# A decoder trunk on one core: work moved between engines at the start, in the last down projection and at the end, and 18 and 15 tiles of weight sums

## Chip, cores and metric

One core of a Trainium2 chip runs the whole program. The metric is the device time of one execution in microseconds; the time given for a kernel is the median of its runs. Engines are named as in the profile: PE (TensorE), DVE (VectorE), ACT (ScalarE), POOL (GpSimd) and SP (SyncE, which issues nearly all DMAs).

## What is computed

x is 2048 tokens by 1024; one layer, fp32 throughout.

```python
mod = (silu(c) @ ada_w + ada_b); sh1, sc1, g1, sh2, sc2, g2 = split(mod, 6)
h = rmsnorm(x, norm1_g) * (1 + sc1) + sh1
x = x + g1 * hybrid_mixer(h, ...)       # w_in 1024 x 4624, SSD scan by chunks of 128, gMLP, w_out 2048 x 1024
h = rmsnorm(x, norm2_g) * (1 + sc2) + sh2
x = x + g2 * conv_gated_ffn(h, ...)     # ff_up 1024 x 5632, causal conv of width 3, silu, ff_down 2816 x 1024
return rmsnorm(x, final_g)
```

## The kernel before

The tokens go in four blocks of 512 (b = 0 to 3, four tiles t of 128). `mixer(b)` runs for each block, and after each odd one `ffn(s)` runs for two blocks at once (s = 0, 1). Each engine's program is written out by hand, in order, with semaphores between them; an engine that waits holds all that is behind it, and SP's order of DMAs is part of it.

A product in fp32 is made of fp32r parts: a weight tile of 128 x 512 is loaded (`w_raw`), ACT rounds it to `w_hi` (`split`, L750), POOL subtracts (`low`, L646), and PE takes hi x hi, hi x lo and lo x hi. One such tile with four 128-wide steps of the other operand is a unit: 12 matmuls of 512 columns. A ring of four slots holds the units. In mixer 0 the split weights are also stored to DRAM (`store_split`), and mixers 1 to 3 load them back, 512 KB a unit (`hl_d`, L378). A mixer has 104 units: 24 for x, B and C of the SSD part (j = 0 to 2, with a conv on DVE after each eight), 32 for the gMLP inputs with the four chunks of the scan between them, 16 for z, 32 for the output projection (j = 0, 1).

The ffn uses a seven-product scheme for 2 x 2 blocks (P1 to P7). For it, POOL makes 33 tiles of weight sums (`t_step`, four subtractions or additions, L657) from four loads each, and SP stores them (`t_store`): tiles 0 to 21 for the up, 22 to 32 for the down projection. `T_OF` says that 20 of them are made in mixer 1 and 13 in the first up projection, `T_AT` at which unit each is loaded. The up projection has 154 units, the down projection 77 (P1, P2, P6, P7, P4, P5, P3 with 11 each); there both the weight and the activation (`a_high` on ACT, `low` on DVE, L1469) are split.

The start: x and small rows are loaded by ACT's queue, the adaLN weights (`ada_w`, slabs of 1 MB) by SP's. DVE multiplies the slabs by silu(c) and adds them (`ada_sum`, L1112), PE sums over partitions into columns (`mod_column`, L1770), and h_hi and h_lo of the first block follow from them (`h_tiles` on ACT; `h_lo` by POOL for the first `HF0` = 4, L664, by `h_lows` on DVE for the rest). The dt projection (L1864) comes after the first eight units.

The end of mixer 0: gate rows of the adaLN weights are summed, PE adds them up (L2022), DVE adds the bias (L1436), and only then `norm_x` takes the statistics of the next block and scales it (L1057 to L1096), for the transposes on PE (L1761).

The end of the program: POOL multiplies y by the gate (`final_step`, L678), DVE adds it to x, takes bn statistics, makes the reciprocal root in 12 small steps (`rms_rstd`); for half 1 POOL multiplies by the gain and ACT scales, for half 0 DVE does both (L1714), and the tiles are stored.

## Time and profile before

| what | us |
|---|---|
| median of 3 runs (2843.17 to 2851.38) | 2846.13 |
| the profiled execution | 2852.3 |
| its span, from the first to the last instruction | 2850.4 |
| PE busy in it | 2705.3 (95%) |
| DVE, POOL, ACT busy | 1849.8, 1094.9, 983.9 |

In the profile a busy time is that of the records of an engine; matmuls overlap, so PE counts as busy also where it runs slower than it could. The granted clock is a share of full speed (1.00 is 2.4 GHz, 0.50 is 1.2 GHz). Stretches are named by their start and end in us from the span's start.

### The profile page before, as it was taken

What the parts mean: (1) busy time and instruction counts of PE and PEld (TensorE: products, weight loads), DVE (VectorE), ACT (ScalarE), POOL (GpSimd) and SP (SyncE); (2) the same over time, 40 slices, a digit from 0 to 9 for tenths busy, and PEclk for the clock granted to TensorE, in tenths of its full rate; (3) what the DMA queues carried; (4) which work ended last, traced back from release to release, by engine and by line L of the source; (5) the groups of instructions that cost most, each with busy time, mean ns of one, the idle gap of its engine ahead of it and who ended that gap; (6) DMA issues with size and microseconds to landing.
All of it is one profiled execution on the core that took longest, in us unless ns stands there. A gap on an engine that the chain in (4) does not pass through costs nothing.

```text
span 2850.4 us, 33659 instructions
## 1 busy us (share of the span) xinstructions
PE 2705.3 (95%) x12363; PEld 2207.4 (77%) x12363; DVE 1849.8 (65%) x2610; ACT 983.9 (35%) x1472; POOL 1094.9 (38%) x736
## 2 busy tenths in 40 slices
PE   3899989899999999999999999999999999999994
PEld 3778868688777888877878888888887888887783
DVE  5777955658467656568786466555737745456868
ACT  2453333322143333344534212233114433334342
POOL 3344431545137777644560000000004544444455
PEclk8899999999999999999999999999999999999997
DMA  9587777999755665573447546665464444437343
GB/s 349 188 299 280 258 266 230 352 350 326 262 183 181 219 210 189 184 280 89 159 153 254 177 156 237 196 221 186 144 225 156 128 126 126 123 110 281 89 131 123
DMA packets 252063, 584.02 MB, mean 205 GB/s; under 512 B 25621, under 2 KB 83449, under 8 KB 247803
## 3 DMA queue, kind: packets, MB, share of 16 engines
q1 hardware_dynamic: 250662, 579.54, 59.9%
q8 instruction: 98, 1.61, 0.2%
q10 hardware_dynamic: 1238, 2.34, 0.2%
q14 instruction: 65, 0.53, 0.1%
HBM read 448.48 MB, written 133.31 MB: 204 GB/s over the span
## 4 chain that ended last, share of the span: by engine, by line
PE 72%; DVE 10%; DMA 7%; POOL 4%; issue 4%; SPq 2%; ACT 1%; DVEq 0%; ACTq 0%; POOLq 0%
PE main L1798 30%; PE pair L2069 14%; PE main L2069 14%; PE main L2083 4%; PE pair L2083 4%; POOL tb L657 2%; DMA t_up_scratch<-tb 2%; DMA tb<-in_ff_up_dram 2%; DVE a_lo L1469 2%; PE pair L1936 1%; DMA w_split_scratch<-w_hl 1%; POOL w_hl L646 1%; DVE mod_sum L1112 1%; SPq L431 1%; SPq L439 1%
## 5 line engine op out<-in xcount | busy, mean ns | idle before, releaser
L646 POOL TENSOR_TENSOR w_hl<-w_raw,w_hl 128x512 fp32r<-128x512 f32 x568 | 828.7, 1463 | 1551.8 <-ACT w_hl L750 1549.5
L750 ACT ACTIVATE w_hl<-w_raw 128x512 fp32r<-128x512 f32 x568 | 355.2, 630 | 867.8 <-PE main L2069 177.8
L1798 PE MATMUL main<-w_hl,h_hi 128*128 128x512 f32 x1536 | 493.6, 403 | 6.3 <-DMA w_hl<-w_split_scratch 5.4
L1798 PEld LDWEIGHTS main<-w_hl,h_hi 128*128 128x128 f32 x1536 | 285.0, 189 | 78.9 <-issue 16.5
L1798 PE MATMUL main<-w_hl,h_lo 128*128 128x512 f32 x768 | 300.9, 392 | 0.0
L657 POOL TENSOR_TENSOR tb<-tb,tb 128x512 f32<-128x512 f32 x132 | 206.2, 1562 | 169.2 <-DMA tb<-in_ff_up_dram 164.5
L1798 PE MATMUL main<-h_hi,w_hl 128*128 128x512 f32 x768 | 250.6, 401 | 11.8 <-POOL h_lo L664 5.4
L1469 DVE TENSOR_TENSOR a_lo<-g,a_hi 128x512 fp32r<-128x512 f32 x132 | 184.1, 1403 | 101.7 <-ACT a_hi L971 101.4
L2083 PE MATMUL main<-w_hl,a_hi 128*128 128x512 f32 x704 | 224.5, 401 | 18.1 <-DVE a_lo L1469 15.4
L2069 PE MATMUL pair<-s_hi,w_hl 128*128 128x512 f32 x736 | 235.7, 393 | 2.4 <-POOL w_hl L646 2.4
L2069 PE MATMUL main<-s_hi,w_hl 128*128 128x512 f32 x672 | 215.5, 394 | 1.9 <-DVE s_lo L1462 1.2
L1532 DVE SCALAR_TENSOR_TENSOR c_acc<-c_gate,col_b,c_acc 128x512 f32<-128x512 f32 x176 | 210.7, 1237 | 3.9 <-ACT c_acc L937 1.5
L1798 PEld LDWEIGHTS main<-h_hi,w_hl 128*128 128x128 f32 x768 | 147.3, 192 | 44.2 <-POOL h_lo L664 5.5
L2083 PEld LDWEIGHTS main<-w_hl,a_hi 128*128 128x128 f32 x704 | 132.8, 192 | 56.7 <-issue 16.7
L1798 PEld LDWEIGHTS main<-w_hl,h_lo 128*128 128x128 f32 x768 | 144.6, 188 | 31.6
L2069 PEld LDWEIGHTS pair<-s_hi,w_hl 128*128 128x128 f32 x736 | 138.2, 188 | 35.5 <-POOL w_hl L646 3.2
L2083 PE MATMUL pair<-w_hl,a_hi 128*128 128x512 f32 x528 | 163.2, 390 | 1.5 <-DVE a_lo L1469 1.3
L1798 PE MATMUL main<-w_hl,gmT_hi 128*128 128x512 f32 x512 | 159.7, 393 | 4.3 <-DMA w_hl<-w_split_scratch 4.3
L2069 PEld LDWEIGHTS main<-s_hi,w_hl 128*128 128x128 f32 x672 | 126.2, 188 | 33.4 <-issue 2.9
L1798 PE MATMUL main<-h_lo,w_hl 128*128 128x512 f32 x384 | 151.9, 396 | 0.0
L1798 PE MATMUL main<-w_hl,yT_hi 128*128 128x512 f32 x480 | 148.5, 390 | 0.0
L2069 PE MATMUL pair<-s_lo,w_hl 128*128 128x512 f32 x368 | 144.6, 393 | 0.0
(268 smaller groups left out, 4908.8 us busy)
## 6 DMA issues: line engine op xcount, KB each, us to landing
w_hl<-w_split_scratch SPq DMA_DIRECT2D x312, 512.0 KB, 3.9
w_split_scratch<-w_hl SPq DMA_DIRECT2D x104, 512.0 KB, 5.8
w_raw<-t_up_scratch SPq DMA_DIRECT2D x176, 256.0 KB, 2.7
w_raw<-in_ff_up_dram SPq DMA_DIRECT2D x132, 256.0 KB, 3.5
w_raw<-t_down_scratch SPq DMA_DIRECT2D x90, 256.0 KB, 2.6
tb<-in_ff_up_dram SPq DMA_DIRECT2D x88, 256.0 KB, 4.6
t_up_scratch<-tb SPq DMA_DIRECT2D x88, 256.0 KB, 5.5
g_scratch<-c_val SPq DMA_DIRECT2D x44, 512.0 KB, 4.0
```

The lines of the kernel that those rows point to most:

```text
L431: sp.dma_start(k_pair(dst), up_quarter(which, t // 2, t % 2)).then_inc(t_ld[m], 16)
L439: sp.dma_start(dst, tb[t_set(t)][which][:]).then_inc(t_st[t_set(t)], 16)
L646: nc.gpsimd.tensor_tensor(w_lo[:, g % RING, :], w_raw[:, g % RING, :], w_hi[:, g % RING, :].bitcast(F32), ALU.subtract).then_inc(w_lo_ok, 1)
L657: nc.gpsimd.tensor_tensor(dst, one, other, how).then_inc(t_add, 1)
L750: nc.scalar.activation(w_hi[:, g % RING, :], w_raw[:, g % RING, :], ACT.Copy).then_inc(w_hi_ok, 1)
L1112: V.scalar_tensor_tensor(out=dst, in0=piece, scalar=c_act[:, k:k + 1], in1=dst, op0=ALU.mult, op1=ALU.add).then_inc(ada_summed, 1)
L1469: V.tensor_tensor(a_lo[j % RING][:], full_a, a_hi[j % RING][:].bitcast(F32), ALU.subtract).then_inc(a_lo_ok, 1)
L1532: last = V.scalar_tensor_tensor(out=piece, in0=c_gate[q % 2][:, i, lo:lo + BT], scalar=col_b[:, R_FW + tap * KF + m:R_FW + tap * KF + m + ...
L1798: ins = T.matmul(main[i], a, w, start=first and p == 0, stop=last and p == 2)
L1936: last = T.matmul(aux[2 + h // (NH // 2)][:, o:o + HD], arow[:, h, :], xdt[:, h * HD:(h + 1) * HD], start=True, stop=True)
L2069: ins = T.matmul(got[:, i, :], w[:, kl, cols], a[:, k, :], start=k == 0 and m == 0, stop=k == KH - 1 and m == 2)
L2083: ins = T.matmul((main, aux)[p % 2][i], a, w[:, s_w, :], start=k == 0 and m == 0, stop=k == KG - 1 and m == 2)
```

## The change

- Start: x is loaded by SP ahead of the adaLN weights. PE multiplies the first two slabs by silu(c) directly (`mod_direct`), so DVE sums six; the columns are made and finished in two halves; h_lo of tiles 0 and 1 is made by DVE, of 2 and 3 by POOL. The dt projection, its transposes, the scan and the second columns each come some units later, and three of the second sums come after the first convs.
- End of mixer 0: `norm_x` comes before the gate rows; PE's sums of these come at unit 11 of j = 0; x and the broadcast gate are loaded four units sooner; all h_lows come after the left half of the residual.
- Weight sums: 18 tiles in mixer 1 (one every 3.6 units instead of 3.2), 15 in the first up projection (one every 8.5 instead of 9.5), stored there six units after their load instead of seven.
- 35 of the weights of the last down projection (P6, one of P7, one of P4, P5 and P3) are loaded, split and stored in mixers 2 and 3 (`pre_load`, `pre_high`, `pre_low`, `pre_store`) and loaded split.
- Odd mixers: the right half of the residual is multiplied by the gate in PSUM and added from there.
- Down projections: four activations are split ahead of the last conv instead of two.
- End: squares with a sum on ACT take the place of the bn statistics; POOL does all multiplications by the gate and the gain, apart from the last quarter, which DVE takes from PSUM; half 0 is scaled on ACT and DVE.

```diff
...
-        ADA_RING, ADA_FIRST, HF0 = 12, 4, 4
+        ADA_RING, ADA_FIRST, HF0, ADA_PE = 12, 4, 2, 2
...
+        PRE_J = list(range(2 * KG, 3 * KG + 1)) + list(range(5 * KG - 1, ND))
...
-        T_OF = (range(0), range(0, 20), range(20, 33))
-        T_AT = ((), [16 + 16 * i // 5 for i in range(20)], [18 + 19 * i // 2 for i in range(13)])
+        PRE_OF = {2: range(17), 3: range(17, len(PRE_J))}
+        PRE_AT = [22 + 17 * i // 5 for i in range(18)]
+        PRE_BUF = 3
+        pre_hi_ok, half_sum, sq_ok = sem("pre_hi_ok"), sem("half_sum"), sem("sq_ok")
+        T_OF = (range(0), range(0, 18), range(18, 33))
+        T_AT = ((), [16 + 18 * i // 5 for i in range(18)], [18 + 17 * i // 2 for i in range(15)])
 
...
+        PRE_G = {ffn0(NSB - 1) + DOWN + j: i for i, j in enumerate(PRE_J)}
...
-                    sp.wait_ge(ada_summed, i - ADA_RING + 1)
+                    sp.wait_ge(mod_col, 1)
...
+            for t in range(NT):
+                sp.dma_start(xn01[:, t, :] if t < 2 else xn23[:, t - 2, :], x[0, t * P:(t + 1) * P, :]).then_inc(x_in, 16)
...
+            def pre_load(i):
+                if i < 2:
+                    sp.wait_ge(t_st[i], 64 * T_IN[i])
+                else:
+                    sp.wait_ge(t_add, T_ADDS + i - 1)
+                sp.dma_start(pre_raw[i % 2][:], down_source(PRE_J[i] // KG, PRE_J[i] % KG)).then_inc(t_ld[i % 2], 16)
+
+            def pre_store(i):
+                sp.wait_ge(t_add, T_ADDS + i + 1)
+                sp.dma_start(pre_d[i], pre_hl[i % PRE_BUF][:].bitcast(F32)).then_inc(hl_st[i % PRE_BUF], 16)
...
+                if b >= 2:
+                    for i, at in zip(PRE_OF[b], PRE_AT):
+                        if n == at + 6:
+                            pre_store(i)
+                    for i, at in zip(PRE_OF[b], PRE_AT):
+                        if n == at:
+                            if i == PRE_OF[3][0]:
+                                sp.wait_ge(x2_st, 16 * NT * 3)
+                            pre_load(i)
                 if b % 2 and 11 <= n < 11 + NT:
...
-                x2_at_unit = OUT + (17 if b else 21)
+                x2_at_unit = OUT + 17
...
-                                if u == at + 7:
+                                if u == at + 6:
...
+                    g = f0 + DOWN + j
+                    if loaded(g):
+                        sp.wait_ge(w_used, g + 1)
+                        sp.dma_start(w_hl[:, g % RING, :, :].bitcast(F32), pre_d[PRE_G[g]]).then_inc(hl_in[g % RING], 16)
+                    else:
+                        load(g, down_source(p, k))
...
+                if loaded(g) or g == UNITS - 1:
+                    return
...
+            def pre_low(i):
+                pool.wait_ge(pre_hi_ok, i + 1)
+                nc.gpsimd.tensor_tensor(pre_hl[i % PRE_BUF][:, 1, :], pre_raw[i % 2][:],
+                                        pre_hl[i % PRE_BUF][:, 0, :].bitcast(F32), ALU.subtract).then_inc(t_add, 1)
...
-                        if j in FIN_AT:
+                        if s + 1 < NSB and j in FIN_AT:
...
+                    for step in range(8):
+                        final_step(s, step)
...
-            for t in range(NT):
-                act.dma_start(xn01[:, t, :] if t < 2 else xn23[:, t - 2, :], x[0, t * P:(t + 1) * P, :]).then_inc(x_in, 16)
...
+            def pre_high(b, n):
+                while b >= 2 and pre_next[0] in PRE_OF[b] and PRE_AT[pre_next[0] - PRE_OF[b][0]] + 3 <= n:
+                    i = pre_next[0]
+                    pre_next[0] += 1
+                    act.wait_ge(t_ld[i % 2], 64 * T_IN[i % 2] + 16 * (i // 2 + 1))
+                    if i >= PRE_BUF:
+                        act.wait_ge(hl_st[i % PRE_BUF], pre_stored(i - PRE_BUF))
+                    nc.scalar.activation(pre_hl[i % PRE_BUF][:, 0, :], pre_raw[i % 2][:], ACT.Copy).then_inc(pre_hi_ok, 1)
+
...
+            def squares(half, c, summed, ts=range(NT)):
+                act.wait_ge(half_sum, summed)
+                for t in ts:
+                    nc.scalar.activation(y_half[half][:, t, c * W:(c + 1) * W], x_half[half][:, t, c * W:(c + 1) * W], ACT.Square,
+                                         accum_out=sq[:, 4 * half + t, c:c + 1]).then_inc(sq_ok, 1)
...
-                    if n == NUP - 1:
+                    if n == NUP - 2:
                         a_high(0)
                         a_high(1)
+                    if n == NUP - 1:
+                        a_high(2)
+                        a_high(3)
...
+                    if s == NSB - 1 and p == P5 and k in (9, 10):
+                        squares(0, 0, 1, (2 * k - 18, 2 * k - 17))
+                    if s == NSB - 1 and p == P3 and k in (6, 7):
+                        squares(1, 0, 2, (2 * k - 12, 2 * k - 11))
+                    if (s, p, k) == (NSB - 1, P3, 8):
+                        squares(1, 1, 3)
...
-            for i in range(3):
-                ada_sum(i)
             for t in range(NT):
                 norm_stats(0, t, (xn01[:, 0, :], xn01[:, 1, :], xn23[:, 0, :], xn23[:, 1, :])[t])
             rms_rstd(NT, xr_ok)
-            for i in range(3, KD):
+            for i in range(ADA_PE, KD):
...
-            mod_columns(0, main[3], R_N1)
-            for i in range(KD, 2 * KD):
+            for half in range(2):
+                mod_columns(0, slice(4 * half, 4 * half + 4), (main[3 - 2 * half], main[2]), R_N1, 1 + half)
...
+                            link(V.tensor_tensor(main[t], main[t], g_bc[:, W:D], ALU.mult))
+                            V.tensor_tensor(x2[:, t, W:D], x2[:, t, W:D], main[t], ALU.add).then_inc(evacuated, 1)
...
+                if b % 2 == 0:
+                    norm_x(b + 1, [xnew[:, t, :] for t in range(NT)])
...
+                        low(s, 2)
+                        low(s, 3)
...
+                    xx = x_half[0][:, t, W:D]
+                    link(V.tensor_tensor(main[t], main[t], g2_bc[:, W:D], ALU.mult))
+                    V.tensor_tensor(xx, xx, main[t], ALU.add).then_inc(half_sum, 1)
...
+                rms_rstd(NT, xr_ok, 0, True)
...
+            def mod_direct(bank):
+
+                for k in range(ADA_PE):
+                    pe.wait_ge(ada_in[k], 16)
                 for m in range(2 * KD):
-                    last = T.matmul(bank[:, m:m + 1], mod_sum[:, 2 * n + m // KD, (m % KD) * P:(m % KD + 1) * P], ones,
-                                    start=True, stop=True)
-                last.then_inc(mod_col, 1)
+                    for k in range(ADA_PE):
+                        T.matmul(bank[:, m:m + 1], ada_t[:, (k + ADA_FIRST) % ADA_RING, m * P:(m + 1) * P], c_act[:, k:k + 1],
+                                 start=k == 0, stop=k == ADA_PE - 1)
 
             pe.sem_inc(w_used, RING)
...
-                        if (j, k) == ((0, 1) if b else (0, KD - 1)):
+                        if (j, k) == ((0, 1) if b else (1, 1)):
...
+                        if b == 0 and (j, k) == (1, 7):
+                            pe.wait_ge(ada_summed, 2 * KD - ADA_PE)
+                            mod_column(1, range(KD), aux[0])
...
-                        if b == 0 and j == 1 and k == 0:
+                        if b == 0 and j == 0 and k == 11:
...
+                def down_weights(u):
+                    if loaded(u):
+                        pe.wait_ge(hl_in[u % RING], 16 * ((NB - 1) * (MU // RING) + PRE_G[u] // RING + 1))
...
```

## Rows read from the trace of the kernel before

**Rows 1.** Windows: busy of PE, PEld, DVE, ACT, POOL; clock, DMA share, GB/s:

```profile
82.76:95.52 12.76, 6.58 (x17) 5.24 (x18) 5.77 (x6) 4.74 (x7) 0.08 (x1) 0.73 0.29 104
95.52:152.15 56.63, 54.15 (x246) 44.75 (x244) 35.81 (x73) 26.78 (x42) 22.42 (x16) 0.91 0.63 204
...
379.10:443.95 64.85, 55.66 (x242) 43.88 (x241) 37.52 (x63) 16.20 (x26) 18.76 (x14) 0.92 0.59 203
443.95:805.39 361.44, 347.84 (x1653) 282.95 (x1652) 218.03 (x402) 94.15 (x132) 126.24 (x82) 0.99 0.88 309
...
1241.94:1470.72 228.78, 219.09 (x957) 176.75 (x957) 176.32 (x176) 104.99 (x174) 137.50 (x89) 0.99 0.50 165
...
1811.80:2152.88 341.08, 341.08 (x1653) 281.75 (x1652) 186.44 (x403) 93.95 (x132) 3.10 (x2) 1.00 0.60 199
...
2588.69:2817.00 228.31, 218.45 (x924) 175.40 (x924) 173.42 (x154) 89.20 (x153) 124.66 (x81) 0.98 0.46 151
2817.00:2850.30 33.30, 0.00 (x0) 0.00 (x0) 28.57 (x54) 4.60 (x4) 10.60 (x4) 0.57 0.31 126
```

**Rows 2.** Chain in order of time: start, us, what, matmuls:

```profile
2690.63 29.92 PE pair L2083 x132
```

**Rows 3.** Waits of PE: total us, times, longest:

```profile
PE main L2083 <- DVE a_lo L1469: 15.4, 17, 2.9
PE main L1798 <- DMA w_hl<-w_split_scratch: 13.6, 11, 2.5
PE pair L1761 <- DVE xnew L1096: 9.2, 1, 9.2
```

**Rows 4.** Timeline of DVE and PE at the start: start, us, what [idle before]:

```profile
22.45 1.29 DVE L1057 BATCH_NORM_STATS2 stats<-xn 128x6 f32<-128x512 f32 x2 [6.75 <-DMA xn<-in_x_dram]
...
30.97 13.82 DVE L1112 SCALAR_TENSOR_TENSOR mod_sum<-ada_t,c_act,mod_sum 128x2048 f32<-128x2048 f32 x5
...
44.84 6.99 PE L1770 MATMUL main<-tri,mod_sum 128*128 128x1 f32 x32 [5.50 <-DVE mod_sum L1112]
57.27 0.80 PE L1798 MATMUL main<-h_hi,w_hl 128*128 128x512 f32 x1 [5.43 <-POOL h_lo L664]
```

**Rows 5.** Windows at the start, columns as in rows 1:

```profile
3.00:30.00 27.00, 0.00 (x0) 0.00 (x0) 13.06 (x22) 0.00 (x0) 0.00 (x0) 1.00 1.01 408
...
35.00:62.00 27.00, 15.37 (x65) 13.98 (x65) 13.46 (x8) 8.20 (x13) 17.89 (x8) 0.68 1.02 416
```

**Rows 6.** Timeline at the end of mixer 0:

```profile
384.90 1.47 DVE L1436 TENSOR_TENSOR gate_rows<-pair,gate_rows 1x512 f32<-1x512 f32 x2 [20.24 <-PE pair L2022]
...
399.50 3.65 PE L1761 MATMUL pair<-ident,xnew 128*128 128x128 f32 x16 [9.19 <-DVE xnew L1096]
```

**Rows 7.** Waits of SP in mixer 1: total us, times, longest:

```profile
SPq L431 <- DMA t_up_scratch<-tb: 41.8, 11, 5.7
```

**Rows 8.** Groups: DVE in mixer 3 and last down projection; POOL, ACT before 443:

```profile
L1366 DVE TENSOR_TENSOR y_sb<-y_sb,stage 128x512 f32<-128x512 f32 x8 | 5.0, 684 | 0.0
...
L1469 DVE TENSOR_TENSOR a_lo<-g,a_hi 128x512 fp32r<-128x512 f32 x45 | 64.8, 1446 | 34.4 <-ACT a_hi L971 34.3
...
L646 POOL TENSOR_TENSOR w_hl<-w_raw,w_hl 128x512 fp32r<-128x512 f32 x104 | 166.3, 1604 | 253.3 <-ACT w_hl L750 251.5 <-DMA w_split_scratch<-w_hl 1.4
...
L750 ACT ACTIVATE w_hl<-w_raw 128x512 fp32r<-128x512 f32 x104 | 64.7, 628 | 158.6 <-PE main L1798 79.4 <-DMA w_split_scratch<-w_hl 61.5 <-issue 17.6
```

**Rows 9.** DVE at a down projection's start; windows of the last one:

```profile
1248.61 3.45 DVE L1469 TENSOR_TENSOR a_lo<-g,a_hi 128x512 fp32r<-128x512 f32 x2
...
2650.00:2690.00 40.00, 36.91 (x152) 27.51 (x151) 35.53 (x37) 14.50 (x26) 18.00 (x13) 1.00 0.31 86
...
2745.00:2817.00 72.00, 68.11 (x289) 54.46 (x287) 58.07 (x43) 25.39 (x44) 52.06 (x28) 0.98 0.43 150
```

**Rows 10.** Timeline of DVE and POOL in the tail:

```profile
2821.11 10.60 POOL L687 TENSOR_TENSOR x_half<-x_half,fg_bc 128x1024 f32<-128x1024 f32 x4 [8.14 <-DVE rstd L1073]
...
2842.11 4.87 DVE L1714 SCALAR_TENSOR_TENSOR x_half<-x_half,rstd,fg_bc 128x1024 f32<-128x1024 f32 x4
```

More of the change, by code:

```diff
@@ L696, in _ @@
                 s = b // 2 - 1
+                if b == NB:
+                    for i in range(len(PRE_J)):
+                        pre_low(i)
                 if b % 2 == 0:
@@ L1249, in mixer @@
                         kx = 4 * j + i
+                        if b == 0 and (j, i) == (0, 2):
+                            dt_copy()
+                        if b == 0 and (j, i) == (1, 2):
+                            scan()
                         full(j, i)
@@ L1255, in mixer @@
                         dt_first()
+                        for i in range(KD + 5, 2 * KD):
+                            ada_sum(i)
+                        dve.wait_ge(a_exp, 1)
+                        link(V.tensor_scalar(small[:, 0, :], small[:, 0, :], -1.0, None, ALU.mult))
                         dt_rest()
-                        scan()
+                        dve.wait_ge(wdt_h, 2)
+                        link(V.memset(state[:], 0.0))
                     if b == 0 and j == 1:
                         acs_copy()
-                        mod_columns(1, aux[0], R_N2)
+                        mod_columns(1, slice(0, KD), (aux[0],), R_N2, 3)
                         for g in range(2):
@@ L1436, in mixer @@
                         V.tensor_tensor(row, aux[m][0:1, :], row, ALU.add).then_inc(gate_ok, 1)
-                if b % 2 == 0:
-                    norm_x(b + 1, [xnew[:, t, :] for t in range(NT)])
-                if b == 0:
-                    h_lows(1, range(4), aux, [acc[:, 0, :], acc[:, 1, :]])
                 dve.wait_ge(x2_in, 16 * (NT + 1) * (b + 1))
```

282 lines of the change are left out of this document (173 added, 109 removed).

## The prediction

> **What bounds the kernel now.** I read the stages first [rows 1]. The span, 2850.4 us, is TensorE's: in mixers 2 and 3 it is busy for all of 341.08 us. A unit is 12 matmuls; a run of 132 in the chain took 29.92 us, so 11 units at 2.72 us [rows 2]. So I look for time in which PE does not run at that pace. Five places hold it. The start: the first unit of the input projection begins at 57.27. The rest of mixer 0: 12.76 us between its first 8 units and the next one, of which the dt matmul is the work, and 64.85 us for its last 16 units. Mixer 1: 361.44 us against 341.08. The two down projections: 228.78 and 228.31 us for 77 units, which are 77 x 2.72 = 209.4. And the tail: 33.30 us after the last matmul [rows 1]. The waits name who ends three of them [rows 3]: a_lo from DVE (15.4 us in the downs), weights from the split scratch (13.6), xnew from DVE (9.2).
>
> **The start.** x (2 MB) is issued on ACT's queue beside 8 MB of adaLN weights, and DVE meets it at 22.45; then it has 5 sums left, 13.82 us from 30.97; after them 32 one-column matmuls take 6.99 us, and h_hi and h_lo another 5.43 until 57.27 [rows 4]. After the change x lands first. The queues move 408 to 416 GB/s [rows 5], so 2.1 MB take 5 us from about 4; its statistics, 8.5 us from 22.45 to 30.97 now, end at 17.5. Slabs 2 to 7 then arrive every 2.5 us until about 29.5, and a sum costs 2.8 (13.82 / 5) at most, so the sums end one after the last landing: about 32 in place of 44.8. Half of the column matmuls (8 of them, 1.7 us), three small ops (0.6), h_hi (0.8), h_lo (1.7) make 37: 20 us sooner. The direct matmuls for slabs 0 and 1 (32, at 6.99 us or less) and the row transposes run in PE's idle time before 31; even rows that land at 30 as now only bring this to about 44.
> But the queue takes over. It is full until 62 [rows 5]: 2.1 + 8.4 + 1.1 + 4.2 MB, then a weight (0.26), a split store (0.52) and a slab (1.05) for each of four units. By that the weights of units 4 to 7 land at about 45, 50, 54, 58, which the new order does not move. Unit 7 then starts at 58.3 + 0.63 + 1.6 (split on ACT and POOL [rows 8]) = 60.5 and ends at 63.2. Units 8 to 10 land at 64, 66, 68 behind the last slab and ws, and ACT evacuates the banks only after the split of unit 10: unit 8 starts at 69. It started at 95.52, after the dt matmul; that follows now at unit 9, 3.6 us at full clock, so I compare 69 + 3.6 = 72.6: 23 sooner.
> From there 56.63 us held 16 units, 43.5, and the same small transposes and columns, 7.3 [rows 1]; of the other 5.8 a 2.5 us wait goes (the scan now sits between two conv tiles, done 6 us before PE asks). Against that: PE idle from 63 to 69 starts unit 8 at the low clock, as it did behind the present gap (a granted mean of 0.73 there, and half is 1.2 GHz) [rows 1], 3.4 us, and the sums 13 to 15, now behind the conv tiles, end within 2 us of PE's call. Net 23 + 2.5 - 3.4 = **22**; bounds 12 (conv and dt work pushes DVE so far that the mixer's chunks begin late) and 27.
>
> **The end of mixer 0.** The statistics and scaling of xnew start only when the gate rows are done and end at 399.36; PE stands 9.19 us, then runs at half clock [rows 6]. Without that the part is 43.5 + two transposes of 2.4 + 1.3 = 49.6 against 64.85. The work (some 11 us: the 8.5 of statistics and four scalings) now starts at 364.7, when DVE falls idle for 20.24 us [rows 6]; hidden by it, it ends at 376. SP has to wait 4 us for the gate rows with three weights queued behind it; they have 8 us of cover. The residual of the left half now stands ahead of the first h_lows, and the broadcast lands at about 388: last h_low at 405, PE asks at 404. Gain 15 - 2 = **13**; bounds 5 and 15.
>
> **Mixer 1.** 20 tiles of weight sums become 18, 4 MB less of 112, and a tile comes every 3.6 units in place of 3.2. SP waited 41.8 us for the stores of a tile before it could load the next into the same buffers [rows 7]; the weights behind those waits are the 13.6 us of PE [rows 3]. The wider step gives a store 2.3 us more and ends most of the first wait. But 10 of the loads now fall on the unit of a store, against 3 before: 2 MB and a weight, 6.2 us at the rate of rows 5 and more until it lands, where the weight has three units, 8.2. I take **5** of the 20.4 us; bounds -5 and 12. The first up projection gets 15 tiles: POOL needs (8.5 + 4) x 1.6 = 20 of 8.5 x 2.72 = 23.1 us per tile [rows 8] and PE has 2.7 units of cover; the store one unit sooner holds SP about 4 us for POOL's last step, with a slack of 1.4 units left. **0**, bounds -2 and 0.
>
> **Mixers 2 and 3, the new work.** 35 down weights are loaded, split and stored: 35 x 0.63 us on ACT and 35 x 1.6 on POOL [rows 8], with 27 MB on queues at 0.6 [rows 1]. ACT waits in order for a load that SP issued three units before; before each evacuation it has at least one unit of cover. POOL is idle there. **0**, bounds -8 and 0. DVE's TENSOR_TENSOR takes 0.68 us in mixer 3 with POOL idle, and 1.45 in the last down projection with POOL at work [rows 8]. The Trainium skill (SBUF — State Buffer, Who interferes with whom) states that such an op with two SBUF inputs and a POOL op block each other for the whole instruction; the trace agrees. By that rule the new subtractions could push DVE in mixers that have no slack on PE: a rival below.
> The residual of odd mixers is multiplied in PSUM: three adds with two SBUF inputs, 0.68 to 1.45 each by those rows, go to 0.68, on the path to the next transposes: 0 to 2.3, **1.3** twice, since POOL is at work there.
>
> **The down projections.** a_lo 2 waited for the conv, collect and gate of the last quarter: it ran at 1248.61 for PE's unit at 1247.2 [rows 9], a stall of 2.9 and half clock behind it, 4.9 us. Now four a_lows stand ahead (to 1243); next late is the weight of unit 3, split after fsilu, at about 1250.9 against 1249.9. **3.5** each; bounds 0 and 4.9. In the second one 35 of 77 weights come split, and POOL is out of DVE's way in P6, where DVE is busy 89% and PE issues 152 matmuls in 40 us, 5.5 us short at 0.2267 each (2.72 / 12), and in P5 and P3, 289 in 72 us, 6.5 us short [rows 9]. I take **11.5** of 12; bounds 4 and 13, since POOL still does the multiplications by the gate there.
>
> **The tail.** POOL takes 10.60 us for four gains, beside which DVE's multiplications and adds of y are slow; the statistics follow, and DVE's last scale is 4.87 from 2842.11; the last store lands some 3 us behind it [rows 10]. New, from the last bank: multiply and add from PSUM 1.4 (2 x 0.68), square 0.6, the chain of the root 2.4 (estimate: the 8.5 of rows 4 less four tiles' statistics), the left half on ACT and the right on DVE 2.5 each, side by side (half of 4.87), store 2.9: 10 with semaphores. The squares of that bank stand behind half1_scale on ACT, and that behind six gains on POOL (2.65 each, from about 15 us before the end): 16. I take 14: **19** of 33.3; bounds 14 and 23.
>
> **Sum.** 22 + 13 + 5 + 0 + 0 + 2.6 + 3.5 + 3.5 + 11.5 + 19 = 80. From the profiled execution (2852.3, span 2850.4) that is 2772; its time is 6 above the median of 2846.1, so 2766 to 2772 and I say **2768**.
>
> **Rivals.**
> The serial parts move less: the start and mixer 0's end at their lower bounds, since DVE, ACT and SP run in order there: 22 + 13 becomes 17, so 2786. For: three programs are reordered at once. Against: the DMA queue, not they, sets unit 7.
> POOL in the way: each of the 35 subtractions (1.6 us) delays DVE by 1.3 us on a path to PE, 46 us: 2814. For: no PE slack in mixers 2 and 3. Against: in mixer 1 POOL is busy 126 us and PE waits for DMA alone [rows 1, 7].
> The split ahead buys nothing: DVE, not POOL, bounds P6 and P3: 11.5 falls away, 2780. For: DVE at 89%. Against: twofold times beside POOL [rows 8].
> Slower: SP meets 70 new issues in order; a pre_store waits for POOL, which waits for ACT, and every weight behind it is late. In mixer 1 a tile of sums cost 20.4 / 20 = 1.0 us of PE. Here the price would have to be over 80 / 35 = 2.3 us; at one whole unit, 2.72, it is 95: 2862. Against: mixer 1 had its queues at 0.88, here they go to about 0.7.
>
> **Chances.** Forecast 62%, less at the serial parts 16%, nothing from the split ahead 12%, POOL 5%, slower 2%, a gain beyond my upper bounds 3%. The range 2750 to 2796 reaches over the first three; POOL, slower and the gain beyond are the 10% left out, and as much again may lie in the tails of the others. Faster by over 0.3% (what a measurement of this kernel tells from no change) 0.96, within 0.02, slower 0.02.
>
> **What would show it.** First unit of the input projection near 37 to 44, the eighth near 60; the chunks of mixer 0 from about 130 in place of 152; no 9 us wait for xnew; mixer 1 near 356; mixers 2 and 3 at 341 to 343; down projections near 225 and 213; a tail of 14. A mixer 2 or 3 above 350, or a start over 50, makes it wrong.

## The result, and the profile after

| | median us (runs) | ratio to before, 95% interval |
|---|---|---|
| before | 2847.05 (4: 2843.17 to 2851.38) | |
| changed | 2815.28 (4: 2811.02 to 2823.99) | 0.9892, 0.9864 to 0.9920 |

The change makes the kernel 1.1% faster. The forecast was 2768, range 2750 to 2796: the direction was right, the size was not. Of 80 us that the sum counted, 37 came.

The windows of the changed kernel by stage, to be set against [rows 1] (length, busy of PE, PEld, DVE, ACT, POOL, clock, DMA share, GB/s). In order: start, rest of mixer 0 up to its output projection (two lines), that projection, mixer 1, first up, first down, mixers 2 and 3, second up, second down, tail:

```profile
0.00:43.02 43.02, 21.66 (x116) 21.23 (x116) 23.57 (x41) 10.22 (x15) 6.03 (x12) 0.97 0.95 369
43.02:136.37 93.35, 87.21 (x372) 71.27 (x373) 65.29 (x95) 41.84 (x65) 40.60 (x25) 0.89 0.74 268
136.37:320.83 184.46, 178.18 (x889) 144.42 (x889) 151.35 (x246) 78.66 (x120) 77.88 (x49) 1.00 0.75 267
320.83:426.60 105.77, 100.77 (x457) 80.01 (x456) 71.74 (x118) 31.22 (x51) 42.50 (x29) 0.98 0.76 275
426.60:783.51 356.91, 345.62 (x1653) 282.16 (x1652) 219.12 (x404) 94.17 (x132) 111.13 (x74) 1.00 0.85 301
783.51:1233.97 450.46, 436.30 (x1881) 347.67 (x1880) 281.85 (x242) 173.44 (x255) 305.29 (x216) 1.00 0.59 195
1233.97:1461.05 227.08, 218.52 (x958) 175.19 (x957) 174.70 (x176) 103.80 (x172) 136.52 (x89) 1.00 0.50 166
1461.05:1802.13 341.08, 341.08 (x1654) 281.67 (x1653) 220.86 (x452) 95.48 (x139) 26.62 (x17) 1.00 0.71 241
1802.13:2143.21 341.08, 341.08 (x1653) 281.62 (x1652) 192.14 (x405) 103.92 (x150) 30.31 (x20) 1.00 0.72 241
2143.21:2575.75 432.54, 429.82 (x1881) 349.76 (x1880) 256.72 (x241) 174.75 (x255) 214.31 (x155) 1.00 0.42 130
2575.75:2801.29 225.54, 216.00 (x925) 175.42 (x923) 161.11 (x161) 81.19 (x144) 97.46 (x53) 0.98 0.57 197
2801.29:2813.70 12.41, 0.00 (x1) 0.00 (x0) 6.13 (x19) 4.71 (x12) 0.00 (x0) 0.65 0.63 251
```

Read against the same stretches of before (the lengths that [rows 1] does not hold are from the same view), with the term of the sum beside it:

| stage | before | after | saved | forecast |
|---|---|---|---|---|
| up to the chunks of mixer 0 | 152.2 | 136.4 | 15.8 | 22 |
| mixer 0, chunks to output projection | 180.3 | 184.5 | -4.2 | 0 |
| output projection of mixer 0 | 111.5 | 105.8 | 5.7 | 13 |
| mixer 1 | 361.4 | 356.9 | 4.5 | 5 |
| first up projection | 436.6 | 450.5 | -13.9 | 1.3 |
| first down projection | 228.8 | 227.1 | 1.7 | 3.5 |
| mixers 2 and 3 | 682.2 | 682.2 | 0.0 | 0 |
| second up projection | 435.8 | 432.5 | 3.3 | 1.3 |
| second down projection | 228.3 | 225.5 | 2.8 | 15 |
| tail | 33.4 | 12.4 | 21.0 | 19 |
| sum | | | 36.7 | 80 |

36.7 is the difference of the spans, 2850.4 - 2813.7. Two stages hold most of what is missing: the first up projection (15.2) and the second down projection (12.2); mixer 0 as a whole gives 17.3 in place of 35.

The waits of PE, of the whole changed kernel (total us, times, longest), beside [rows 3]:

```profile
PE main L2246 <- DVE a_lo L1606: 12.4, 14, 4.2
PE pair L2226 <- POOL w_hl L703: 7.6, 13, 2.3
...
PE main L2226 <- POOL w_hl L703: 4.8, 9, 1.4
PE pair L1903 <- ACT xn L808: 4.7, 1, 4.7
```

The wait for xnew is gone. New are the waits of the up projection (L2226) for weights, 12.4 us in all, where before had 3.0. And a_lo still holds PE for 12.4 us, against 15.4, in another place: 8.5 us of it lie in four waits of the last product, one of 4.2.

In the last product of the down projection (P3) the timelines of DVE and POOL show how:

```profile
2777.18 4.49 DVE L1813 TENSOR_TENSOR x_half<-x_half,y_half 128x2048 f32<-128x2048 f32 x1
2781.60 2.83 DVE L1606 TENSOR_TENSOR a_lo<-g,a_hi 128x512 fp32r<-128x512 f32 x1
2784.35 4.45 DVE L1813 TENSOR_TENSOR x_half<-x_half,y_half 128x2048 f32<-128x2048 f32 x1
2788.72 5.59 DVE L1606 TENSOR_TENSOR a_lo<-g,a_hi 128x512 fp32r<-128x512 f32 x2
...
2761.46 12.43 POOL L735 TENSOR_TENSOR y_half<-y_half,g_bc 128x1024 f32<-128x1024 f32 x4 [23.53 <-DVE y_half L1763]
2773.85 19.92 POOL L746 TENSOR_TENSOR x_half<-x_half,fg_bc 128x1024 f32<-128x1024 f32 x6
```

POOL works without a gap for 32.3 us, and an a_lo that takes 0.69 alone takes 2.8. DVE is then busy end to end, PE waits, and the window of P3, before and after, says what it cost:

```profile
2780.56:2816.99 36.43, 32.60 (x133) 25.43 (x131) 31.03 (x24) 11.38 (x20) 27.33 (x14) 0.95 0.32 113
...
2757.44:2801.29 43.85, 35.33 (x133) 27.08 (x131) 41.79 (x33) 14.76 (x29) 32.31 (x10) 0.88 0.49 173
```

### The profile page after: what moved, and what is told of

Same layout as the page of the kernel before. It is cut to its first block, busy times and chain, and to the rows that moved or that the text cites. A ratio compares the mean times of both kernels' runs of the same rounds, so it can differ in the third digit from the quotient of the medians.

```text
span 2813.7 us, 33836 instructions
## 1 busy us (share of the span) xinstructions
PE 2716.2 (97%) x12427; PEld 2210.4 (79%) x12427; DVE 1824.6 (65%) x2589; ACT 993.4 (35%) x1505; POOL 1088.7 (39%) x737
## 4 chain that ended last, share of the span: by engine, by line
PE 66%; DVE 10%; issue 6%; POOL 6%; DMA 6%; SPq 1%; ACT 1%; DVEq 0%; POOLq 0%; ACTq 0%
PE main L1956 28%; PE pair L2226 12%; PE main L2226 10%; PE pair L2246 6%; PE main L2246 4%; POOL w_hl L703 3%; DMA w_split_scratch<-w_hl 2%; POOL tb L714 2%; DVE a_lo L1606 1%; PE pair L2093 1%; DMA tb<-in_ff_up_dram 1%; DVE stats L1167 1%; PE pair L2118 1%; PE pair L2078 1%; DMA w_hl<-w_split_scratch 1%
## 5 line engine op out<-in xcount | busy, mean ns | idle before, releaser
L703 POOL TENSOR_TENSOR w_hl<-w_raw,w_hl 128x512 fp32r<-128x512 f32 x532 | 766.8, 1447 | 917.3 <-ACT w_hl L818 912.0
L818 ACT ACTIVATE w_hl<-w_raw 128x512 fp32r<-128x512 f32 x532 | 331.8, 630 | 827.9 <-DMA w_raw<-t_up_scratch 152.8
L751 POOL TENSOR_TENSOR pre_hl<-pre_raw,pre_hl 128x512 fp32r<-128x512 f32 x35 | 53.9, 1544 | 563.4 <-ACT pre_hl L842 563.4
L714 POOL TENSOR_TENSOR tb<-tb,tb 128x512 f32<-128x512 f32 x132 | 195.1, 1478 | 182.5 <-DMA tb<-in_ff_up_dram 178.3
L1606 DVE TENSOR_TENSOR a_lo<-g,a_hi 128x512 fp32r<-128x512 f32 x132 | 176.3, 1345 | 105.1 <-ACT a_hi L1071 104.7
L2226 PE MATMUL pair<-s_hi,w_hl 128*128 128x512 f32 x736 | 237.0, 394 | 6.6 <-POOL w_hl L703 6.6
L2246 PE MATMUL main<-w_hl,a_hi 128*128 128x512 f32 x704 | 222.3, 397 | 15.6 <-DVE a_lo L1606 12.4
L2226 PE MATMUL main<-s_hi,w_hl 128*128 128x512 f32 x672 | 217.2, 395 | 5.8 <-POOL w_hl L703 4.3
L1669 DVE SCALAR_TENSOR_TENSOR c_acc<-c_gate,col_b,c_acc 128x512 f32<-128x512 f32 x176 | 204.6, 1202 | 10.8 <-ACT c_acc L1037 8.5
L2226 PEld LDWEIGHTS pair<-s_hi,w_hl 128*128 128x128 f32 x736 | 138.1, 188 | 42.8 <-issue 6.0
L2226 PEld LDWEIGHTS main<-s_hi,w_hl 128*128 128x128 f32 x672 | 126.1, 188 | 40.7 <-issue 8.0
```

Of the source, the lines that this page charges most:

```text
L703: nc.gpsimd.tensor_tensor(w_lo[:, g % RING, :], w_raw[:, g % RING, :], w_hi[:, g % RING, :].bitcast(F32), ALU.subtract).then_inc(w_lo_ok, 1)
L714: nc.gpsimd.tensor_tensor(dst, one, other, how).then_inc(t_add, 1)
L751: nc.gpsimd.tensor_tensor(pre_hl[i % PRE_BUF][:, 1, :], pre_raw[i % 2][:], pre_hl[i % PRE_BUF][:, 0, :].bitcast(F32), ALU.subtract).then_i ...
L818: nc.scalar.activation(w_hi[:, g % RING, :], w_raw[:, g % RING, :], ACT.Copy).then_inc(w_hi_ok, 1)
L1606: V.tensor_tensor(a_lo[j % RING][:], full_a, a_hi[j % RING][:].bitcast(F32), ALU.subtract).then_inc(a_lo_ok, 1)
L1669: last = V.scalar_tensor_tensor(out=piece, in0=c_gate[q % 2][:, i, lo:lo + BT], scalar=col_b[:, R_FW + tap * KF + m:R_FW + tap * KF + m + ...
```

## Experiments

Each kernel is the changed one with the edit shown; each has four runs, and the ratio is to the kernel before on the same chip. Several chips were used, so the ratios, not the times, compare one experiment with another. First units, and with them the stages up to the chunks of mixer 0, scatter: over the profiles of kernels with the same start, the first unit lay at 43.0 to 47.3 and the chunks began at 131.7 to 136.4. So a stage of its own profile is compared where one stage is meant.

**The weight sums: four runs.** Four things are disputed at once (store one unit sooner, 15 tiles, every 8.5 units, 18 tiles in mixer 1).

```diff
-                                if u == at + 6:
+                                if u == at + 7:
                                     t_store(t)
```

> The changed kernel with one edit: in the first up projection each tile of weight sums is stored seven units after its load, as before the change, not six; 18 and 15 tiles stay. Theory A (the earlier store holds SP until POOL's last sum, and the weight behind it comes late): SP's wait for POOL's sums there falls from 102 us to 45 to 60, the first up projection from 450.5 us to 436 to 439, PE's waits for w_hl from 11.7 us to under 3, and the whole is 12 to 14 us shorter than the changed kernel, about 2802. Theory B (15 tiles, one every 8.5 units, are too much for POOL): the up projection stays at 446 to 451.

Measured: ratio 0.9856 (0.9841 to 0.9871), 2809.95. The up projection took 446.3, SP's wait for the sums 58.7. So the earlier store costs something (4 to 9 us; the profiles of kernels that keep the changed schedule gave 450.5 to 454.9), but it is not the whole loss: neither theory held alone.

```diff
-        T_OF = (range(0), range(0, 18), range(18, 33))
-        T_AT = ((), [16 + 18 * i // 5 for i in range(18)], [18 + 17 * i // 2 for i in range(15)])
+        T_OF = (range(0), range(0, 20), range(20, 33))
+        T_AT = ((), [16 + 16 * i // 5 for i in range(20)], [18 + 19 * i // 2 for i in range(13)])
```

> The changed kernel with one edit: 20 tiles of weight sums in mixer 1 (one every 3.2 units) and 13 in the first up projection (one every 9.5), as before; the store stays at six units there. Theory A: the up projection stays long, 13/15 of its loss, 446 to 450 us. Theory B: it falls to 436 to 439. For mixer 1: if 18 tiles brought its gain of 4.5 us, it goes from 356.9 back to 360 to 362; if what comes ahead of it did, it stays at 357.

Measured: 0.9844 (0.9829 to 0.9859), 2806.83; up projection 439.7, mixer 1 359.1. The larger part of the loss went, so number or spacing was the larger part; mixer 1 takes 2 us more with 20 tiles. Both edits together:

> The changed kernel with the schedule of weight sums of before in whole: 20 tiles in mixer 1, 13 in the first up projection, stored seven units after their load. The two runs that undid one half each left the up projection at 446.3 and 439.7 us against 450.5. Theory A and B together (both the number and the earlier store cost): it falls to 436 to 438, mixer 1 goes to 359 to 361, and the whole is 13 to 16 us shorter than the changed kernel. Rival (something else in the change, as the start or the earlier loads, shifts the up projection): it stays above 439.

Measured: 0.9834 (0.9810 to 0.9857), 2800.64; up projection 435.4, mixer 1 359.2. The changed kernel on the same chip took 2815.55, so 15 us come back: the whole loss is in the schedule of the sums. It left open whether 15 tiles are too many or only too close:

```diff
-        T_AT = ((), [16 + 18 * i // 5 for i in range(18)], [18 + 17 * i // 2 for i in range(15)])
+        T_AT = ((), [16 + 18 * i // 5 for i in range(18)], [18 + 9 * i for i in range(15)])
...
-                                if u == at + 6:
+                                if u == at + 7:
```

> The changed kernel with 18 and 15 tiles kept, stored seven units after the load in the first up projection, and one tile every 9 units there in place of 8.5 (the last at unit 144). The same with 8.5 took 446.3 us in the first kernel of this study. Theory J (the spacing is what costs: at 8.5 every second tile is loaded eight units after the one before, one unit behind its store, and the weights of those units wait behind both): the up projection falls to 435.5 to 439 with all 15 tiles, mixer 1 stays at 357. Rival B (the number of tiles is POOL's limit): 15/13 of the work still costs, 444 to 447.

Measured: 0.9831 (0.9810 to 0.9853), 2803.27; the up projection took 435.4 with all 15 tiles. In the up projection the number costs nothing, the spacing of 8.5 does. Some of the price went to the stage behind it: the last tile is now loaded at unit 144 and stored at 151 of 154, and the first product of the down projection took 34.9 us, with a wait of 2.9 for a split weight, where the profiles with other schedules of the sums have 31.1 to 32.3. The windows of the up projection of the four kernels, in the order told:

```profile
781.56:1227.87 446.31, 434.67 (x1881) 348.26 (x1881) 282.14 (x241) 174.01 (x255) 307.81 (x215) 1.00 0.60 196
...
782.93:1222.63 439.70, 432.73 (x1881) 350.48 (x1880) 278.14 (x242) 174.88 (x255) 300.94 (x208) 1.00 0.57 190
...
787.65:1223.03 435.38, 430.81 (x1882) 349.49 (x1881) 285.10 (x243) 174.59 (x255) 300.63 (x208) 1.00 0.58 192
...
787.85:1223.29 435.44, 430.84 (x1881) 349.45 (x1880) 284.21 (x241) 172.57 (x252) 304.25 (x214) 1.00 0.61 201
```

POOL is busy 301 to 308 us in all of them, under 70% of the stage: its busy time alone does not set the stage. SP's waits for POOL's sums in that stage, in the changed kernel, then stored at seven, then every nine:

```profile
SPq L464 <- POOL tb L714: 102.2, 15, 7.9
...
SPq L464 <- POOL tb L714: 58.7, 15, 4.3
...
SPq L464 <- POOL tb L714: 56.3, 15, 4.8
```

The last two are alike, and yet they are 11 us apart. What differs is how long ACT waited for the DMA of weights: 154 us at 8.5 (stored at seven) and 108 at nine, beside 187 in the changed kernel and 75 in the kernel before.

Theory J gives as the reason that at 8.5 every second tile is loaded one unit behind the store of the one before. That can't be it in the changed kernel: stored at six, the load stands two units behind, as it does at nine stored at seven, and yet the spacing costs the same 11 us there (450.5 against 439.7). In time the two distances come out alike, as the rows of SP show; here for two tiles of the changed kernel (L464 stores, L458 loads):

```profile
1098.24 1.78 SPq L464 DMA_DIRECT2D t_down_scratch<-tb  x4
...
1102.67 1.76 SPq L458 DMA_DIRECT2D tb<-in_ff_down_dram  x4
...
1122.56 1.80 SPq L464 DMA_DIRECT2D t_down_scratch<-tb  x4
...
1126.98 1.76 SPq L458 DMA_DIRECT2D tb<-in_ff_down_dram  x4
```

All tiles of this projection use one set of buffers (`t_set`), so a load waits until the store before it has landed. It went out 4.3 to 4.5 us behind it, as soon as that, in twelve of fourteen cases both in the changed kernel and with the store at seven, and in seven of fourteen at nine units; the store went out about 20 us behind its own load. From the second load to the last a tile took 24.4 us in the changed kernel and 24.1 with the store at seven, where PE's pace would make it 23.1 (8.5 units of 2.72); at nine units it took 24.9 (pace 24.5), at 9.5 from 25.9 to 26.3 (25.8). This fits a round of load, sums, store and landing that 8.5 units are too short for. No run gives the tiles a second set of buffers, so it is not shown apart.

**P3: POOL beside DVE.**

```diff
                 for n, (half, c) in enumerate(((0, 0), (1, 0), (1, 1))):
                     pool.wait_ge(sq_ok, NT * (n + 1))
+                    if n == 1:
+                        pool.wait_ge(a_lo_ok, (s + 1) * ND)
```

> The changed kernel with one wait more: POOL's last four multiplications by the final gain (half 1) start only when DVE has made the last a_lo. Theory C (a POOL op and a DVE op with two inputs in SBUF hold each other up, and POOL's row of ten such ops is what makes P3 long): a_lo's in P3 take 1.4 us or less once POOL is silent, P3 goes from 43.9 us to 33 to 37, the tail from 12.4 to 14 to 17, the whole 3 to 7 us shorter than the changed kernel. Rival D (DVE's own adds of 4.5 us in order ahead of the a_lo's make P3 long, POOL or not): P3 stays over 40 and the whole gets longer by what the tail gets.

Measured: 0.9874 (0.9858 to 0.9889), 2815.35. The windows of P3 and the tail, and DVE's steps behind the last a_lo (POOL's four gains ran from 2788.30 to 2797.66):

```profile
2759.93:2793.44 33.51, 30.83 (x133) 24.28 (x131) 32.45 (x20) 10.08 (x24) 23.19 (x9) 1.00 0.56 194
2793.44:2815.78 22.34, 0.00 (x0) 0.00 (x0) 15.07 (x32) 9.28 (x16) 4.22 (x2) 0.59 0.47 188
...
2786.88 1.28 DVE L1608 TENSOR_TENSOR a_lo<-g,a_hi 128x512 fp32r<-128x512 f32 x2
...
2788.47 2.26 DVE L1182 TENSOR_SCALAR rstd<-ms 128x4 int32<-128x4 int32 x1
2790.76 2.31 DVE L1185 TENSOR_TENSOR rt<-rstd 128x4 f32<-128x4 f32 x1
2793.11 2.27 DVE L1186 SCALAR_TENSOR_TENSOR rt<-rt,ms 128x4 f32<-128x4 f32 x1
2795.41 2.26 DVE L1188 SCALAR_TENSOR_TENSOR rstd<-rt,rstd 128x4 f32<-128x4 f32 x1
2797.71 0.16 DVE L1185 TENSOR_TENSOR rt<-rstd 128x4 f32<-128x4 f32 x1
```

Theory C holds: with POOL silent the last a_lo's are back at 0.64 and P3 falls from 43.9 to 33.5, 10.4 us. The expected gain of the whole did not come, since the tail grew by 9.9: DVE's chain of small steps met the same four POOL steps, and each step of four elements a partition then lasted as long as one POOL instruction, 2.3 us in place of 0.16. The price was moved, not paid off.

```diff
-                for n, (half, c) in enumerate(((0, 0), (1, 0), (1, 1))):
+                for n, (half, c) in enumerate(((0, 0), (1, 0))):
...
                     rms_rstd(NT, r1_ok, 4, True)
...
+                    for t in range(NT):
+                        xx = x_half[1][:, t, W:D]
+                        V.scalar_tensor_tensor(out=xx, in0=xx, scalar=rstd[:, 4 + t:5 + t], in1=fg_bc[:, W:D],
+                                               op0=ALU.mult, op1=ALU.mult).then_inc(y0_free, 1)
```

> The changed kernel with two of POOL's six multiplications by the final gain taken away (right half of half 1) and done by DVE in one step with the scale, four of 0.69 us after its last a_lo; ACT scales the left half only. Theory C (POOL beside DVE): POOL's row in P3 is 6.6 us shorter, P3 goes from 43.9 us to 37 to 40, the tail stays at 12.4 to 14.5, the whole is 3 to 6 us shorter. Rival (what one engine is relieved of the other pays, as when the gains were only made late): within 1.5 us of the changed kernel.

Measured: 0.9879 (0.9854 to 0.9904), 2815.61, no difference to the changed kernel that its runs could show (0.9882 beside it), as the rival had it. By its profile (its fastest run, 2808.12; the four reach to 2818.86) P3 fell by 5.9 us, as expected, and the tail grew by 3.5, more than expected:

```profile
2752.53:2790.50 37.97, 33.09 (x133) 26.07 (x131) 36.46 (x32) 12.65 (x28) 25.19 (x8) 0.91 0.51 186
2790.50:2806.39 15.89, 0.00 (x0) 0.00 (x0) 9.52 (x24) 5.45 (x12) 0.00 (x0) 0.64 0.57 227
```

**The split ahead.**

```diff
-        PRE_J = list(range(2 * KG, 3 * KG + 1)) + list(range(5 * KG - 1, ND))
+        PRE_J = list(range(5 * KG - 1, ND))
...
-        PRE_OF = {2: range(17), 3: range(17, len(PRE_J))}
+        PRE_OF = {2: range(11), 3: range(11, len(PRE_J))}
```

> The changed kernel with only 23 weights split ahead in mixers 2 and 3: those of P6 and the first of P7 are split in the last down projection as before. Theory F (the split ahead takes POOL out of DVE's way in P6, worth 5.3 us there): P6 goes from 30.0 us back to 34 to 36, all else alike, the whole 4 to 6 us longer. Rival G (the four a_lo ahead at the start of the down projection are what made P6 fast): P6 stays at 30 to 31.

Measured: 0.9902 (0.9879 to 0.9926), 2820.79, 5.2 us above the changed kernel beside it. P6 took 34.64; in the changed kernel 30.04:

```profile
2635.56:2670.20 34.64, 32.14 (x133) 24.24 (x133) 30.34 (x31) 12.27 (x22) 15.10 (x11) 1.00 0.29 84
...
2636.84:2666.88 30.04, 30.04 (x133) 24.61 (x132) 18.97 (x27) 7.25 (x12) 1.99 (x2) 1.00 0.60 196
```

POOL's 11 subtractions (15.1 us) cost DVE 11 us of busy time; without them PE runs through. The product ahead of it (P2) goes back too, from 29.9 to 31.0, as before the change. Theory F holds, and the rival with the four a_lo ahead falls.

**The start.** The edit moves ACT's scaling of x ahead of its two copies of the transposed rows.

> The changed kernel with ACT scaling x (four tiles, 4.3 us) before it copies the transposed rows out of PSUM, not after. Theory E (at the start ACT waits 26 us for the rows that PE transposes behind its 64 direct matmuls, and x's scaling, ready at 17.6, waits with it): PE's wait of 4.7 us for xn goes, the first unit starts at 38 to 39 in place of 43.0. Then if only the order of the engines bounds what follows, the ninth unit starts 4.7 us sooner than at 71.5; if the DMA queue does (the weight of the eighth unit landed at 59.0), only 2 to 3 us, and the whole gains 2 to 3.

Measured: 0.9883 (0.9866 to 0.9900), 2818.93. PE's rows at the start, first of the changed kernel, then with the edit:

```profile
14.45 13.79 PE L1924 MATMUL main<-c_act,ada_t 128*128 128x1 f32 x64 [11.89 <-DMA ada_t<-in_ada_w_dram]
33.45 3.61 PE L1903 MATMUL pair<-ident,xn 128*128 128x128 f32 x16 [4.74 <-ACT xn L808]
36.88 3.72 PE L1914 MATMUL main<-tri,mod_sum 128*128 128x1 f32 x32
43.02 0.79 PE L1956 MATMUL main<-h_hi,w_hl 128*128 128x512 f32 x1 [2.41 <-DVE h_lo L1198]
...
29.65 3.67 PE L1903 MATMUL pair<-ident,xn 128*128 128x128 f32 x16 [0.51 <-ACT col_b L808]
33.12 6.83 PE L1914 MATMUL main<-tri,mod_sum 128*128 128x1 f32 x32
42.35 0.79 PE L1956 MATMUL main<-h_hi,w_hl 128*128 128x512 f32 x1 [2.40 <-DVE h_lo L1198]
```

The wait of 4.7 us is gone, but the columns now run at half the pace (6.83), so the first unit hardly moves. In the five profiles in which the columns were as slow without the edit, the first unit lay at 46.1 to 47.3: against these the edit gives 3.8 to 5.0. The ninth unit starts at 71.0, against 72.5 to 73.7 there. At the chunks nothing of it is to be seen: they begin at 135.2, against 134.7 to 136.0 (the four of them that leave the second columns alone). This fits the theory that the DMA queue, not the engines, sets the first units; the whole shows no gain.

**The changed kernel once more.**

> The changed kernel itself once more, beside the other three, to see how far its stages vary from run to run: span of the stages within 2 us of the first profile, the first up projection at 450 to 455 us, P3 at 43 to 44.5, the time within 0.2% of 0.989 of the kernel before.

Measured: 0.9882 (0.9861 to 0.9903), 2815.55; first up projection 453.5, P3 44.1, first unit 46.4 (outside the 2 us), chunks at 135.3.

**The second columns.** The edit changes `(j, k) == (1, 7)` to `(2, 0)` for `mod_column(1, ...)`.

> The changed kernel with PE's second set of 16 columns of the adaLN sums one unit later (after unit 16 instead of 15). Theory H (in mixer 0 the three sums that the change put behind the first convs reach PE 3.5 us late, and PE then runs the columns and three units at the low clock): the wait falls to about 1 us, the columns take 5 us in place of 7, and the first chunk of the mixer's second part starts at 129 to 133 in place of 135 to 136.4; the whole 3 to 5 us shorter. Rival (DVE's and SP's work behind the columns takes it back): the first chunk starts at 135 or later.

Measured: 0.9894 (0.9873 to 0.9916), 2814.20. Of the changed kernel, then with the edit:

```profile
102.66 6.99 PE L1914 MATMUL pair<-tri,mod_sum 128*128 128x1 f32 x32 [3.47 <-DVE mod_sum L1225]
...
100.59 4.81 PE L1914 MATMUL pair<-tri,mod_sum 128*128 128x1 f32 x32
```

The wait is gone, the columns take 4.8 in place of 7.0, and the chunks begin at 132.9. But a wait of 2.4 us for a weight came in its place, and three kernels without the edit reached 131.7, 131.8 and 132.7: in the scatter of the start the gain is not shown.

**The first four h_lo of block 1.**

```diff
+                if b == 0:
+                    h_lows(b + 1, range(4), aux, [acc[:, 0, :], acc[:, 1, :]])
...
                 residual_left()
...
-                    h_lows(b + 1, range(KD), aux, [acc[:, 0, :], acc[:, 1, :]])
+                    h_lows(b + 1, range(0 if b else 4, KD), aux, [acc[:, 0, :], acc[:, 1, :]])
```

> The changed kernel with the first four h_lo of block 1 made by DVE before the left half of the residual of mixer 0, not after it. Theory I (the residual waits until 385.8 for the broadcast gate, so h_lo comes late to PE's second transposes, which take 5.5 us in place of 1.9): the output projection of mixer 0 takes 102 to 103 us in place of 105.8. Rival: the residual, later by 6 us, is in the way of the last bank, and nothing is gained.

Measured: 0.9877 (0.9863 to 0.9892), 2811.81; the output projection of mixer 0 took 101.5 in place of 105.8 (104.2 to 107.1 in all profiles of changed kernels without the edit, 100.9 and 101.5 in the two later ones with it). Theory I holds, with 4.3 us by these two profiles; on the whole time it is within the scatter of the runs.

**Together.**

> The changed kernel with four edits together: weight sums scheduled as before the change (as in the fifth kernel), the right half of half 1 scaled with its gain by DVE (as in the sixth), the second columns one unit later, and the first four h_lo of block 1 ahead of the residual. If the causes are separate, their gains add: 15 + 8.5 (by the sixth kernel's profile) + 4 + 3 = 30 us less than the changed kernel's 2815, about 2787 to 2792; if the tail takes back what P3 gains, about 2795.

Measured: 0.9805 (0.9790 to 0.9820), 2791.37. Its windows of first up, second down and tail:

```profile
778.88:1213.83 434.95, 430.41 (x1881) 349.63 (x1881) 282.38 (x244) 174.44 (x255) 300.41 (x208) 1.00 0.58 192
...
2554.50:2775.10 220.60, 213.80 (x925) 174.47 (x923) 155.68 (x160) 79.07 (x143) 90.05 (x51) 0.98 0.59 200
2775.10:2790.90 15.80, 0.00 (x1) 0.00 (x0) 9.44 (x24) 5.45 (x12) 0.00 (x0) 0.65 0.57 226
```

It is 24 us below the changed kernel. The expectation of 30 counted the sixth kernel at 8.5, which was mostly where its profiled run happened to lie; with its 2.4 by stages, and 15 and 4.3 for the sums and the h_lo, the sum is 22, and up to 4 more for the columns, whose gain is not shown. It is the fastest version of the study, with the next one beside it:

> The kernel with four edits, but with 18 and 15 tiles, one every 9 units in the up projection and stored at seven. If theory J holds, mixer 1 gives 2.3 us more than with 20 tiles and the up projection nothing back: 2787 to 2790, against 2791.4. If B holds: 2797 to 2800.

Measured: 0.9798 (0.9779 to 0.9816), 2792.63: the two cannot be told apart. The up projection took 435.3 with 15 tiles, mixer 1 359.1, against 359.5 with 20 tiles, so the 2 us that 18 tiles seemed to give mixer 1 did not show here (361.2 in the run with a tile every nine units, 355.4 to 357.3 in the others with 18). Both kernels with a tile every nine units ran on a chip of their own, and mixer 1 is the same program in all that have 18 tiles, so the chip may be in these 2 to 4 us.

## Why the prediction was wrong, step by step

**The first up projection, -13.9 measured; the sum had 0 for its weight sums and 1.3 for the residual in PSUM.** The step that failed was: "the store one unit sooner holds SP about 4 us for POOL's last step, with a slack of 1.4 units left. **0**, bounds -2 and 0." The hold was about right (SP's wait went from 47.7 to 102.2 us, 3.7 a tile to 6.8); the slack was not there. It was counted for one weight with everything else on time, while the tile's own loads, its store and the gate's store are issued by the same SP. And the bound on the other edit, POOL's 20 of 23.1 us per tile, tested the engine's capacity alone; the landing of the store, for which the next load waits in the same buffers, 4.4 us behind its issue, had no term. Whether that landing or the shared SP makes 8.5 units too short stays open. The runs with one of the two halves undone gave 446.3 and 439.7, both undone 435.4, and 15 tiles every nine units 435.4. The 1.3 for the residual fits: with the sums as before this stage is 1.2 us shorter than before the change, and the second one, which has no sums, 3.3; no run tests it apart.

**The second down projection, 15 forecast, 2.8 measured.** "I take **11.5** of 12" held where its reason held. P6 went from 34.7 to 30.0 (shown by undoing it: 34.6 again), and P2 from 31.0 to 29.9. The step that failed is that P5 and P3 would gain too, 6.5 us short as they were: P5 gave 0.3, P3 lost 7.4. The first product, 36.1 to 31.2, belongs to the other 3.5 of the 15. The split ahead took POOL's subtractions out of P3, but the change puts ten steps of 1024 elements in their place, 32.3 us without a gap, where there were four such among the subtractions, 27.3 us. The forecast named the multiplications by the gate, and let them only lower the gain to its bound of 4; the six gains stand in it as "that behind six gains on POOL", as a delay of the end, never as a neighbour of the a_lo's. In this P3 a_lo took 2.35 us in the mean, against 0.69 beside a silent POOL. The Trainium skill (SBUF — State Buffer, Who interferes with whom) gives the lock between POOL and a DVE instruction with two inputs in SBUF, and the trace agrees with it. The forecast used the rule for mixers 2 and 3, where it cost nothing, and not for the end, where it decides.

**Mixers 2 and 3, 0 forecast, 0.0 measured.** The rival with POOL in DVE's way there is refuted: 341.08 us twice, with 27 and 30 us of POOL. DVE was slowed (215.8 to 220.9 and 186.4 to 192.1 busy), but had the time. The same fact sank the rival of late weights. That the time of the whole, 2815, lies beside the 2814 of the rival with POOL in the way is chance: what that rival describes did happen, but in P3 and not in the mixers for which it was priced.

**The start, 22 forecast, 15.8 measured (within its bounds of 12 and 27).** The forecast for the first unit, 37 to 44, held at 43.0, at its late end. Its step "the direct matmuls for slabs 0 and 1 (32, at 6.99 us or less)" was wrong by two: 64 rows, 13.79 us, behind which the rows' transposes and x's scaling stood until 33.45. That cost nearly nothing, since, as forecast, the queue takes over: weights of units 4 to 7 landed at 45.9, 50.3, 54.6 and 59.0, against 45, 50, 54 and 58, and the ninth unit came at 71.5 against 69. What failed was "the sums 13 to 15 ... end within 2 us of PE's call": 3.5 us, and PE paid for the gap again at half clock, 6.99 for the columns (granted clock 0.50) and 3 more over the next two units.

**Chunks of mixer 0, no term, -4.2.** PE waits there for v_sb (2.1), bcT (1.6) and three lesser ones, 6.2 us in all in place of 3.3. The kernels of the study all have 184 to 186, so it belongs to the change. What makes the waits longer stays open: DVE and ACT are busy for 151.4 and 78.7 us, against 150.5 and 78.1 before, so it is not more work on them, and no run tests it apart.

**The end of mixer 0, 13 forecast, 5.7 measured.** "Without that the part is 43.5 + two transposes of 2.4 + 1.3 = 49.6 against 64.85." The 64.85 held the eight gate matmuls, 3.6 us; the change moves them, and the sum took them for gone. The second wait was forecast at 2 us: the broadcast gate landed 65.0 us after the start of the stage, not 55.5, and the transposes took 5.5 for 1.9, which is 3.6; undone it gave 4.3. A wait of 1.7 for ACT's evacuation is new.

**Mixer 1, 5 forecast, 4.5 measured.** The size is right, the reason only in part: with 20 tiles the changed kernel still takes 359.1 to 359.5, against 361.4 before, so about half of it is not the sums'; what it is no run separates. And with 18 tiles the profiles have 355.4 to 361.2, so the other half is not shown either.

**The tail, 19 forecast, 21.0 measured,** and 12.4 us long against 14: the last squares waited for nothing, since PE's late end had given POOL the time to be done. The gain of the tail and the loss of P3 are one account: POOL's steps are early because they run beside P3. Without them there (third experiment) P3 and tail take 55.9 us, with them 56.3. The forecast priced one side. Of the forecast's rivals none described this.

**The a_lo's ahead, 3.5 each.** First products: 34.8 to 31.7 and 36.1 to 31.2, 3.1 and 4.9. In the first down projection P5 took 36.2 in this profile and 36.1 in one other, but 34.5 to 34.9 in the remaining twelve, so 1.7 is a low reading of it.

The two largest errors share a form: the range, 2750 to 2796, took its bounds from each edit beside unchanged neighbours. Both losses arise where a moved or respaced step meets work that its edit did not touch.

## What to carry to other kernels

Price a moved step where it lands as carefully as where it leaves: name which instructions of the other engines run beside it, and take their durations with it, not without it; here ten POOL steps turned a tail's gain of 21 us into 14. A periodic load, sum and store has to be tested by its whole round, from one load to the next with the landing of the store in it, not by the busy share of one engine: 15 tiles cost the up projection nothing at nine units apart and 11 us at eight and a half (that the round is the reason fits the rows, and is not shown apart). And a difference of two stage lengths is a saving only if what left the stage is gone: moved work has to be put on the other side at once.
